# First modulation weights in two halves of channels, with the first projection's products between the halves

## The reference, cut to what matters

```python
c_act = jax.nn.silu(c)
mod = jnp.einsum('bd,de->be', c_act, w_ada[l]) + b_ada[l]      # 1024 -> 6 * 1024
sh1, sc1, g1, sh2, sc2, g2 = [m[:, None, :] for m in jnp.split(mod, N_ADA, axis=-1)]
h = rmsnorm(x, norm_mix_g[l]) * (1.0 + sc1) + sh1
proj = jnp.einsum('bsd,de->bse', h, w_in[l])                   # 1024 -> 1280
```

## Time and profile before

| what | value |
| --- | --- |
| median of three runs | 2007.48 us (2007.09 to 2008.2) |
| the profiled execution | 2007.32 us |
| its span | 2005.5 us |
| TensorE busy | 1942.7 us, 97% |
| VectorE, ScalarE, POOL busy | 917.9, 724.0, 10.5 us |
| moved from and to memory | 346.43 MB |

### The profile page before, as it was taken

How to read it: one execution, slowest core, us unless ns; L and a number is a source line. 1 busy time by engine, 2 the same in 40 slices (tenths; PEclk the granted TensorE clock), 3 DMA queues, 4 the chain that set the end, 5 groups by cost and what they waited for, 6 DMA issues and landing times.

```text
span 2005.5 us, 23835 instructions
## 1 busy us (share of the span) xinstructions
PE 1942.7 (97%) x9831; PEld 1333.3 (66%) x9831; DVE 917.9 (46%) x1487; ACT 724.0 (36%) x1197; POOL 10.5 (1%) x21
## 2 busy tenths in 40 slices
PE   6999999999999899999999999999998899999999
PEld 4756643333333267767788887877787678888787
DVE  4375412222111145574466665335555356666533
ACT  4365211111111141675343333235443643333323
POOL 1000000000000000000000000000000000000000
PEclk8999999999999999999999999999999999999999
DMA  9678479999999941401133332222222023332211
GB/s 322 147 279 224 192 296 427 428 428 428 427 427 427 424 142 42 138 1 37 49 109 101 97 93 98 92 86 69 77 67 60 22 64 99 91 105 84 105 64 42
DMA packets 168038, 346.43 MB, mean 173 GB/s; under 512 B 19643, under 2 KB 142267, under 8 KB 152443
## 3 DMA queue, kind: packets, MB, share of 16 engines
q1 hardware_dynamic: 165907, 340.85, 46.5%
q10 hardware_dynamic: 1224, 2.15, 0.9%
q0 software_dynamic: 800, 1.91, 0.4%
HBM read 340.70 MB, written 4.19 MB: 172 GB/s over the span
## 4 chain that ended last, share of the span: by engine, by line
PE 87%; DMA 7%; DVE 3%; ACT 2%; issue 1%; SPq 0%; DVEq 0%
PE bank L2106 22%; PE bank L1351 13%; PE bank L2123 12%; PE bank L1920 10%; PE bank L1939 4%; PE bank L1301 2%; PE bank L887 2%; DMA norm_area<-in_w_down 2%; PE bank L908 2%; DMA norm_area<-in_w_up 2%; PE bank L1889 2%; DMA ring<-in_w_up 2%; PE bank L1289 2%; PE bank L931 2%; DMA ring<-in_w_in 1%; PE bank L1365 1%
## 5 line engine op out<-in xcount | busy, mean ns | idle before, releaser
L557 DVE TENSOR_TENSOR ring_low<-ring,w_high 128x2048 fp32r<-128x2048 f32 (+1 forms) x91 | 207.7, 2282 | 125.7 <-ACT w_high L550 125.6
L550 ACT ACTIVATE w_high<-ring 128x2048 fp32r<-128x2048 f32 x90 | 171.3, 1905 | 218.4 <-PE bank L2106 174.0
L2106 PE MATMUL bank<-h_high,ring_low 128*128 128x512 f32 x640 | 249.8, 390 | 0.0
L2106 PE MATMUL bank<-low_ff,w_high 128*128 128x512 f32 x608 | 238.4, 392 | 0.0
L2106 PE MATMUL bank<-h_high,w_high 128*128 128x512 f32 x608 | 236.6, 389 | 0.0
L2123 PE MATMUL bank<-ff_split,w_high 128*128 128x512 f32 x704 | 222.5, 396 | 1.6 <-DVE work L2828 1.6
L2123 PEld LDWEIGHTS bank<-ff_split,w_high 128*128 128x128 f32 x704 | 132.4, 188 | 35.8 <-DVE work L2828 2.4
L2123 PE MATMUL bank<-ff_split,ring_low 128*128 128x512 f32 x352 | 139.3, 396 | 0.0
L2106 PEld LDWEIGHTS bank<-h_high,ring_low 128*128 128x128 f32 x640 | 120.4, 188 | 26.5
L2106 PEld LDWEIGHTS bank<-h_high,w_high 128*128 128x128 f32 x608 | 114.2, 188 | 25.2
L2106 PEld LDWEIGHTS bank<-low_ff,w_high 128*128 128x128 f32 x608 | 114.2, 188 | 24.5
(11 more groups left out here) (456 smaller groups left out, 3376.1 us busy)
## 6 DMA issues: line engine op xcount, KB each, us to landing
ring<-in_ffn_w_up SPq DMA_DIRECT2D x88, 512.0 KB, 5.2
ring<-in_w_gate SPq DMA_DIRECT2D x16, 2048.0 KB, 22.7
ring<-in_w_down SPq DMA_DIRECT2D x12, 2048.0 KB, 26.8
ring<-in_ffn_w_down SPq DMA_DIRECT2D x22, 1024.0 KB, 4.9
ring<-in_w_ada SPq DMA_DIRECT2D x18, 1024.0 KB, 8.2
const<-in_w_gate SPq DMA_DIRECT2D x8, 2048.0 KB, 22.8
work<-in_w_up SPq DMA_DIRECT2D x8, 2048.0 KB, 22.7
ring<-in_w_up SPq DMA_DIRECT2D x8, 2048.0 KB, 23.3
```

Of the source, the lines that this page charges most:

```text
L550: act.activation(high_of(n, words), slab_view(g)[:, 0:words], ACT.Copy).then_inc(sem("split_high"), 1)
L557: dve.tensor_tensor(ring_low[:, slot_of(g), 0:words], slab_view(g)[:, 0:words], high_of(n, words).bitcast(F32), ALU.subtract).then_inc(sem ...
L2106: mm = pe.matmul(bank[n % 6][:, :], st[k], mv[k], start=(k == 0), stop=(k == len(st) - 1))
```

## The change

The eight slabs of `w_ada` columns 0 to 2047 are cut another way. `plan_ada_half(h)` makes four slabs for half h: each holds two k, and of shift and of scale the 512 columns of channels 512h to 512h + 511, loaded in two transfers of 512 KB with rows of 2 KB. The order of loads becomes half 0, w_in's first slab, half 1, w_in's second slab. Slab products become `ada_half_slab`: eight matmuls of 256 columns in the code where `ada_slab` has four of 512, half 0 into bank 4, half 1 into bank 5. The diff below leaves out the hunks that only pass the new step numbers on.

The first four slabs take the TAIL slots and no slab goes to HIGH any more, so the splits into `w_high` wait for no `ada_used`; the ring is filled from slot 0 on and then in the order 1, 2, 3, 4, 0, 5.

Rows, transposes, columns, gain and scaling are made for half 0 (k 0 to 3) and again for half 1 (k 4 to 7). On ScalarE the split of w_in's first slab comes behind the first four `h_high` tiles, and the second slab's behind the other four. On TensorE the order is: half 0's slabs, their transposes, slab 4, high by high for k 0 to 3, slab 5, the products with low h, slab 6, the products with low weights, slab 7, transposes, and then the three kinds for k 4 to 7. The waits of ScalarE, VectorE and POOL for the eighth `ada_used` stay at 8, which now comes behind the products of half 0.

```diff
--- before.py
+++ after.py
@@ -398,7 +399,8 @@
         HIGH_SLOTS, TAIL_SLOTS, H_SLOTS = (RING, RING + 1), range(RING + 2, RING + 6), (RING + 6, RING + 7)
         CONST_SLOTS, NORM_SLOTS = (RING + 8, RING + 9), (RING + 10, RING + 11)
         N_SLOTS = RING + 12
-        EARLY = 6
+        EARLY = 4
+        FIRST_RING, NEXT_RING = (0, 1, 2, 3, 4, 5), (1, 2, 3, 4, 0, 5)
         slot_count = [0] * N_SLOTS
         slot_holds = [None] * N_SLOTS
         loaded_at, before_in_slot = {}, {}
@@ -406,9 +408,9 @@
 
         def slot_of(g):
             if g < EARLY:
-                return (*TAIL_SLOTS, *HIGH_SLOTS)[g]
+                return TAIL_SLOTS[g]
             if not moe_at or g < moe_at[0]:
-                return (g - EARLY) % RING
+                return (FIRST_RING if g < EARLY + RING else NEXT_RING)[(g - EARLY) % RING]
             if g < moe_at[0] + MOE_N:
                 return moe_slots[(g - moe_at[0]) % len(moe_slots)]
             return late_slots[(g - moe_at[0] - MOE_N) % len(late_slots)]
@@ -630,10 +632,19 @@
                 ada_w.append((plan([(v, w_ada[P * k:P * k + P, SLAB * c:SLAB * c + SLAB])], sem("ada_used"), len(ada_w) + 1), v))
 
 
-        plan_ada(0)
+        def plan_ada_half(h):
+            for m in range(TT):
+                v = slab_view(len(slabs)).rearrange("p (k s n) -> p k s n", k=2, s=2)
+                pieces = [(v[:, k], w_ada[P * (2 * m + k):P * (2 * m + k) + P, 0:SLAB].rearrange("p (s n) -> p s n", s=2)[:, :, S * h:S * h + S])
+                          for k in range(2)]
+                ada_w.append((plan(pieces, sem("ada_used"), len(ada_w) + 1), v))
+
 
         w_in = t["w_in"][0]
-        in_u = [plan_cols(w_in, 256 * j, 256, sem("in1_done"), TT * (j + 1)) for j in range(2)]
+        in_u = []
+        for j in range(2):
+            plan_ada_half(j)
+            in_u.append(plan_cols(w_in, 256 * j, 256, sem("in1_done"), TT * (j + 1)))
         in_q = []
         for j in range(2):
             viewed(SLAB, lambda x: x.rearrange("p (k r n) -> p k r n", k=DT, r=2))
@@ -736,7 +747,7 @@
         od_out = [plan_cols(t["od_w_out_2"][0], 512 * j, 512, sem("out3_done"), 4 * (j + 1)) for j in range(2)]
         ffn_w.append(plan_ffn(1))
 
-        IN_SPLIT = split(in_u + in_q + [in_kv], first=[(sem("ada_used"), EARLY - 1 + i) for i in range(2)])
+        IN_SPLIT = split(in_u + in_q + [in_kv], first=[None, None])
         OUT1_SPLIT = split(out1_w)
         EV_SPLIT = split([ev_cq, ev_kv] + ev_dq + ev_dk + ev_dv, third=2, first=[(sem("moe_used"), n) for n in high_free])
         OUT2_SPLIT = split_into(ev_out, (3, 4, 5, 2))
@@ -1702,20 +1713,32 @@
                 c, k = divmod(m, DT)
                 row = silu_0[:, k, (1, 1, 0)[c]:(2, 3, 2)[c]]
                 for j in range(TT):
-                    mm = pe.matmul(bank[ADA_BANK[c > 0]][32 * j:32 * j + row.shape[1], :], row,
-                                   ada_w[m][1][:, S * j:S * j + S], start=(m in (0, DT)), stop=(m in (DT - 1, 3 * DT - 1)))
+                    mm = pe.matmul(bank[ADA_BANK[2]][32 * j:32 * j + row.shape[1], :], row,
+                                   ada_w[m][1][:, S * j:S * j + S], start=(m == DT), stop=(m == 3 * DT - 1))
                 mm.then_inc(sem("ada_used"), 1)
 
-            def ada_turn(part):
-
-                pe.wait_ge(sem("ada_row"), 2 * (part + 1))
-                for q in range(TT):
-                    mm = pe.transpose(bank[ADA_BANK[part]][:, P * q:P * q + 98], mod_row[0:98, part, P * q:P * q + P],
+            def ada_half_slab(m):
+                loaded(pe, ada_w[m][0])
+                h, n = divmod(m, TT)
+                at = slice(HALF * h, HALF * h + HALF)
+                for k in (2 * n, 2 * n + 1):
+                    for j in range(TT):
+                        part, q = divmod(j, 2)
+                        mm = pe.matmul(bank[ADA_BANK[h]][32 * j:32 * j + 1, at], silu_0[:, k, 1:2],
+                                       ada_w[m][1][:, k % 2, part, HALF * q:HALF * q + HALF], start=(k == 0), stop=(k == DT - 1))
+                mm.then_inc(sem("ada_used"), 1)
+
+            def ada_turn(step):
+
+                pe.wait_ge(sem("ada_row"), 2 * (step + 1))
+                part = step // 2
+                for q in range(TT) if part else (2 * step, 2 * step + 1):
+                    mm = pe.transpose(bank[ADA_BANK[step]][:, P * q:P * q + 98], mod_row[0:98, part, P * q:P * q + P],
                                       ident[0:98, 0:98])
                 mm.then_inc(sem("ada_turned"), 1)
 
-            for m in range(DT):
-                ada_slab(m)
+            for m in range(TT):
+                ada_half_slab(m)
                 if m == 0:
                     wide_spread(pe, "mix")
             ada_turn(0)
@@ -1737,22 +1760,36 @@
                     rms_sum(pe, "qk", NORM_QK, i - QK_AT - 1)
 
             begun = in1_tiles[0:4]
-            for k in range(DT):
+
+            def begun_high(k):
                 pe.wait_ge(sem("h1_ready"), k + 1)
                 if k == 0:
                     pe.wait_ge(sem("split_high"), IN_SPLIT + 1)
                 for i, (_, st, mv, m, w) in enumerate(begun):
                     pe.matmul(bank[i][0:m, 0:w], st[3 * k], mv[3 * k], start=(k == 0), stop=False)
-            pe.wait_ge(sem("split_low"), IN_SPLIT + 1)
-            for k in range(DT):
+
+            def begun_low(k):
+                if k == 0:
+                    pe.wait_ge(sem("split_low"), IN_SPLIT + 1)
                 for i, (_, st, mv, m, w) in enumerate(begun):
                     pe.matmul(bank[i][0:m, 0:w], st[3 * k + 1], mv[3 * k + 1], start=False, stop=False)
-            for k in range(DT):
+
+            def begun_rest(k):
                 pe.wait_ge(sem("h1_low"), k + 1)
                 for i, (_, st, mv, m, w) in enumerate(begun):
                     mm = pe.matmul(bank[i][0:m, 0:w], st[3 * k + 2], mv[3 * k + 2], start=False, stop=(k == DT - 1))
                     if k == DT - 1:
                         mm.then_inc(sem("in1_done"), 1)
+
+            ada_half_slab(TT)
+            for n, products in enumerate((begun_high, begun_rest, begun_low)):
+                for k in range(TT):
+                    products(k)
+                ada_half_slab(TT + n + 1)
+            ada_turn(1)
+            for products in (begun_high, begun_low, begun_rest):
+                for k in range(TT, DT):
+                    products(k)
             project_pe(pe, "in1", [0, 1, 2, 3], in1_tiles, after=in1_after, skip=4)
 
             pe.wait_ge(sem("front_loaded"), 32)
@@ -2222,23 +2259,24 @@
             wide_part(act, "mix")
             wide_root(act, "mix")
 
-            def ada_rows(part):
-
+            def ada_rows(step):
+
+                part = step // 2
                 if part:
                     act.wait_ge(sem("pool_cleared"), 3)
-                act.wait_ge(sem("ada_used"), 3 * DT if part else DT)
+                act.wait_ge(sem("ada_used"), ADA_USED[step])
+                at = slice(0, S) if part else slice(HALF * step, HALF * step + HALF)
                 for j in range(2):
                     rows = slice(32 * j, 32 * j + 1 + part)
-                    r = act.activation(mod_row[rows, part, :], bank[ADA_BANK[part]][rows, :], ACT.Copy)
+                    r = act.activation(mod_row[rows, part, at], bank[ADA_BANK[step]][rows, at], ACT.Copy)
                 r.then_inc(sem("ada_row"), 1)
 
-            ada_rows(0)
-            split_act(act, IN_SPLIT)
-
-            for k in range(DT):
-                act.wait_ge(*scaled("mix", k + 1))
-                act.activation(h_high[:, k, :], h_in[:, k, :], ACT.Identity, bias=mod[:, k:k + 1]).then_inc(sem("h1_ready"), 1)
-            split_act(act, IN_SPLIT + 1)
+            for h in range(2):
+                ada_rows(h)
+                for k in range(TT * h, TT * h + TT):
+                    act.wait_ge(*scaled("mix", k + 1))
+                    act.activation(h_high[:, k, :], h_in[:, k, :], ACT.Identity, bias=mod[:, k:k + 1]).then_inc(sem("h1_ready"), 1)
+                split_act(act, IN_SPLIT + h)
             for i, (o, m, w) in enumerate(in1_out):
                 copy_out(act, "in1", i, 4, o, m, w)
                 if i in (3, 7, 9):
@@ -2545,40 +2583,51 @@
             mod_v = mod[:, :].rearrange("p (c j q) -> p c j q", c=ADA_C, j=TT)
             b_v = vec[:, VEC["b_ada"]:VEC["b_ada"] + 48].rearrange("p (c j q) -> p c j q", c=ADA_C, j=TT)
 
-            def ada_rows_dve(part):
-
+            def ada_rows_dve(step):
+
+                part = step // 2
                 if part:
                     dve.wait_ge(sem("pool_cleared"), 3)
                 else:
                     dve.wait_ge(sem("cleared"), 1)
-                dve.wait_ge(sem("ada_used"), 3 * DT if part else DT)
+                dve.wait_ge(sem("ada_used"), ADA_USED[step])
+                at = slice(0, S) if part else slice(HALF * step, HALF * step + HALF)
                 for j in range(2, TT):
```

(62 more changed lines are left out.)

## The result

The changed kernel took 2012.54 us (median of nine runs, 2012.4 to 2013.46), the kernel before 2008.2 us beside it (nine runs, 2006.39 to 2009.74). The ratio is 1.0025, with a 95% interval of 1.0017 to 1.0033: slower by about 5 us, a quarter of a per cent. The experiments ran beside the kernel before as well, at a median of 2007.39 us for the first four and 2007.46 us for the other four, and all ratios leave out slow executions (there was one, of 10.9 ms, beside the first four). The profiled execution has a span of 2010.7 us against 2005.5, 5.2 us more.

The account below looks back on a forecast made before the run. TensorE, busy for 97% of the span, was taken as the bound. The begun tiles' end moves from 50.08 to 55.8 with nothing to absorb it: 2007.32 + 5.7 = 2013.0 us, range 2009.0 to 2017.5.

Parts of the forecast that it names:

- End of half 0's slabs: On TensorE, the first four half slabs, 0.857 us each, three of them from 24.43, end at 27.19.
- First product: Half 0's first product waits for ScalarE's split of w_in's first slab and starts at 34.6, 1.6 us earlier than before.
- First product to slab 7's end: On TensorE, 48 products (5.75 us), three slabs (2.57) and a low clock (1.7) bring slab 7's end to 44.8.
- The wait added: Half 1's chain waits for slab 7; TensorE has a gap of 3.4 us with two transposes, first h_high at 48.2.
- The last 48 products: Half 1's products on TensorE take 5.75 us plus 1.7 for a low clock behind the second gap.
- The end: The last product of the begun tiles ends at 55.8 instead of 50.08, 5.7 us later.
- What is moved past: rel_bias lands at about 53.1, wanted at 59.0, cover 5.9 us; later loads move, eight more SP issues cost nothing.
- The clock that stays up: Rival, chance 0.12: TensorE keeps 2.4 GHz through both gaps, products end at 53.0, +2.9 us, 2010.2.
- Later gaps: Rival, chance 0.07: the shift moves low spells behind TensorE's later waits; two going give back 3.4 us, 2009 to 2011.
- Half slabs as dear as whole ones: Rival, chance 0.06: a 256-column product takes as long as one of 512, six half slabs cost 5.1 us more, 2018.
- Small transfers at 186 GB/s: Rival, chance 0.03: 512 KB pieces of w_ada load that slowly, slab 7 lands at 60.2, products end near 72, 2029.
- moved queue: Rival, chance 0.08: rel_bias or the q weights arrive over 5.9 us later than reckoned, 2014 to 2019.

Follow-up runs that it names:

- the first experiment: Changed kernel with TensorE's order alone altered: slabs 5 to 7 right behind the high products of half 0, half 1's transposes between half 0's products; 2009.04 us, ratio 1.0005.
- third experiments: Changed kernel's loads and half slabs in one pass: eight half slabs, all transposes, then 96 products, w_in's first split behind ScalarE's first rows; 2012.15 us, ratio 1.0023.
- the fourth experiment: Changed kernel with ScalarE's order alone altered: it splits w_in's first slab before copying the rows of half 0; 2006.55 us, ratio 0.9994.
- the second trace: The changed kernel run again unaltered; 2013.05 us, ratio 1.0026.
- the one-pass runs: Half slabs, all transposes, then 96 products, with w_in's first slab loaded ahead of half 1 (2012.15 us) or behind it (2009.17 us).
- The filled trace of the changed kernel: Changed kernel with products whose result nobody reads in both of TensorE's gaps; 2009.33 us, ratio 1.0009.
- fifth: Changed kernel with both orders altered: ScalarE splits w_in's first slab ahead of the rows, TensorE takes slabs 5 to 7 behind half 0's high products; 2004.34 us, ratio 0.9984.
- seventh experiments: Kernel before with products whose result nobody reads in TensorE's gap behind the first modulation slabs; 2006.88 us, ratio 0.9996.

## Why the prediction was right

The forecast was 5.7 us more than the profiled execution of before, 2013.0; the range and the sign held. By the steps, for the changed kernel's first trace:

- *End of half 0's slabs* forecast 27.2, measured 25.86. I kept the low spell of 20.8 to 24.2 that the trace of before has; in this trace the clock was full there and the norm's spread took 1.16 us instead of 1.89. Of the eight further traces, with the same work before it, two show such a spell (the first and third experiments) and six do not, so nothing here speaks for an effect of the change.
- *Slab end to first scale* forecast 2.0, measured 1.91 and 1.88: right.
- *First product* forecast 7.4 us behind the slabs, measured 7.33, with the split of w_in's slab as the last thing waited for. Right, and shown by the fourth experiment: with that split alone out of the way the first product came 3.9 us nearer to the slabs' end.
- *First product to slab 7's end* forecast 10.2, measured 10.68. A low spell of 3.2 us where I took 3.4. At the full clock a slab between products took 0.97 us, not 0.857, and sixteen products 2.1 us, not 1.92.
- *The wait added* forecast 3.4 us, measured 3.44.
- *The last 48 products* forecast 7.6, measured 8.63. This is the one term mis-sized. I gave the second gap a low spell of 3.4 us under work; it was 6.2 us, or 1.4 us more cost, of which the pace of h_high hides a part. In the second trace it was 3.4 us and the products took 7.7.
- *The end* forecast 55.8, measured 55.94: 1.3 us too late at the start and 1.5 too early in the terms behind it cancel. The mechanism was right, but that the end came out within 0.2 us is luck.

*Loading.* I had half 1 landed by 36.4 at the latest; the one-pass run shows 35.2. In the first trace nothing waits for half 1's slabs; in the second, slab 4 held TensorE for 0.6 us inside the first gap, where it cost nothing. What I did not say plainly is that the landing itself came 4.6 us later than before. The change hides loading that it has itself made longer.

*What is moved past.* rel_bias was issued at 45.8 and landed 4.9 us later, at 50.7, and its user L1756 ran at 59.2: a cover of 8.5 us, forecast 5.9. SP issued the ring's pairs for the experts at 190.5, 221.1 and 237.4 instead of 173.4, 200.4 and 231.6, and the transfers still ran dry at 258. Eight more issues cost nothing that shows, though the first eight took SP 1.1 us each and the next eight 1.6, not half a microsecond: the median transfer still landed 11 to 12 us after its issue, so the issues stayed well ahead of the data. From the timeline of the changed kernel:

```profile
45.82 0.53 POOL L1666 DMA_DIRECT2D work<-in_rel_bias  x1
...
59.17 1.02 PE L1756 MATMUL bank<-const,work 33*8 33x512 f32 x2
...
190.53 0.33 SPq L1607 DMA_DIRECT2D ring<-in_w_gate  x1
221.05 0.33 SPq L1607 DMA_DIRECT2D ring<-in_w_up  x1
237.38 0.33 SPq L1607 DMA_DIRECT2D ring<-in_w_gate  x1
```

*The rivals.* The clock that stays up did not happen; where filling the gaps made it happen the end was 52.05 (forecast 53.0), 2.0 us late. Later gaps did shift, but no two spells went (see below). Half slabs as dear as whole ones fell: 48 instructions took 2.77 us where 24 of twice the columns took 2.76. Small transfers at 186 GB/s fell: slabs of half 1 came at 384 in the one-pass runs. No moved queue ended last. The rule cited from the Trainium skill ("TensorE: Matmul & The Clock Gate", "HAM oscillation — how this bites in real kernels"), that each burst behind a wait is met throttled, agrees with both traces of the changed kernel: 0.50 behind both gaps, though in the second trace only from 0.7 us into the last 48 products on. For shorter waits it is not borne out each time: a wait of 2.4 us near 90 us, the same in every trace, is followed by a low spell in seven of the ten.

**How the 5.9 us divide.** With both kernels at a full clock the begun tiles end at 52.05 and 49.90: 2.15 us are the serial steps, that is, the chain gone through twice with a 1.9 us split in it, less the early start. The other 3.7 us are the clock, which costs the changed kernel 3.9 and the kernel before 0.2. The filled trace of the changed kernel began 0.3 us earlier; without that the parts are 2.5 and 3.4. The two are not independent: the low spells stood behind the gaps and were gone where the gaps were filled, and taking away what makes a gap gave back most of its length and its spell (the first experiment for the second gap, the fourth for the first).

*The last 0.7 us.* Behind 655 us (in the kernel before) the shift moves. It falls from 5.9 to 5.3 us by 667, where TensorE's waits for the experts' transfers differ by tenths of a microsecond, and to 4.6 at 901, behind a low spell that only the kernel before has there; the changed kernel has one at 1361.0 to 1364.4 that the other lacks, and there the shift rises to 5.4. Which gap draws a spell thus moved with the 5.9 us, as the rival of the later gaps said, but the sum of it is small. This is read from the traces alone; no run tested it. The windows of the kernel before and of the changed one:

```profile
898.00:901.40 3.40, 3.40 (x10) 1.38 (x8) 1.84 (x2) 2.08 (x7) 0.00 (x0) 0.50 0.00 0
...
903.00:910.00 7.00, 6.06 (x40) 4.07 (x38) 5.67 (x19) 5.51 (x19) 0.00 (x0) 1.00 0.00 0
```

## What to carry to other kernels

Here, cutting a load in halves to start earlier paid only when the second half's small serial steps ran under the first half's work and the first half's path was short: put what produces their input ahead of that work in every engine's order, not behind it. And look for work in the new first path whose input is already there; here one split, moved into idle time of its engine, was worth what the whole change had lost. Price a new gap on TensorE with the lower clock behind it; whether such a spell costs anything depends on what else paces the products.

## What the runs showed of the hardware

- The low spells of one kernel differ between executions: the changed kernel had 3.2 and 6.2 us of work under the low clock in one trace and 5.7 and 3.4 in the other, and ended within 0.4 us. Over ten runs the kernel with ScalarE's split first spread from 2004.0 to 2011.0 us.
- A low clock can be nearly free. The kernel before has 5.0 us of products under it, and a full clock gave back 0.2 us, because h_high and the low split set the pace.
- One and the same wait need not bring a low spell. TensorE waits 2.4 us for ring_low near 90 us in every trace. Seven traces have a spell of 3.4 us behind it; those of the fourth, fifth and seventh experiments have none, and there the shift against the kernel before changes by 1.6 us. These three traces are also the fastest executions of their kernels, so their ends must not be laid to their edits. The kernel before, and the same with its gap filled:

```profile
92.50:95.90 3.40, 3.40 (x9) 2.63 (x8) 2.46 (x2) 0.00 (x0) 0.00 (x0) 0.51 0.47 50
...
92.00:96.00 4.00, 4.00 (x19) 3.23 (x18) 2.77 (x2) 0.00 (x0) 0.00 (x0) 1.00 0.48 53
```

- The clock can stay down for long: in the one-pass kernel, where TensorE first got short bursts of slabs and then the products, it was at 1.2 GHz from 31.3 to 44.9 us with TensorE busy for 8.4 us of that.

```profile
31.40:44.90 13.50, 8.42 (x53) 5.15 (x54) 6.65 (x14) 5.26 (x9) 7.58 (x14) 0.50 1.11 274
```
